# The shift-vector add of the first two layer norms issued on Pool instead of the Vector engine

## The chip, the cores and the metric

One Trainium2 chip, eight NeuronCores. Every core runs the same program on its own two sequences of the batch of sixteen; no data passes between cores. The metric is device time in microseconds (us) of the slowest core. PE is the matrix engine (PEld its weight loads), DVE the Vector engine, ACT the Scalar engine, Pool the GpSimd engine, SP the engine whose queue carries most DMAs.

## The reference

One layer of a streaming encoder, width 1024, sequences of 2048 tokens. Cut to what matters:

```python
def layer_norm(x, g, b):
    mu = mean(x, -1); var = mean((x - mu) ** 2, -1)
    return (x - mu) * rsqrt(var + EPS) * g + b          # b is the shift vector

h = x
mix = hybrid_mixer(h)          # in-projection, attention heads | SSD heads, then W_out
h = layer_norm(ALPHA * h + mix, ln1_g, ln1_b)
xa = memory_cross_attention(h, mem)                     # 4 heads over 256 memory tokens
h = layer_norm(ALPHA * h + xa, ln2_g, ln2_b)
ffn = hierarchical_moe(h)      # top-1 group, top-2 experts of it
h = layer_norm(ALPHA * h + ffn, ln3_g, ln3_b)
```

## The kernel before

Each core takes its two sequences one after the other through four stages: the in-projection with its convolutions (called P2 in the code's names), attention and SSD scan together (P3 to P5), the out-projection with the first normalisation (P6), and cross-attention with the second normalisation and the router (P7). The expert stage for both sequences together and the third normalisation follow. A sequence is 16 tiles of 128 tokens, and a tile of the residual is 128 partitions x 1024 float32 in `arenaH`; the gain vector `lng` and the shift vector `lnb` lie in SBUF, repeated on all partitions.

Every engine works through its own queue in the order in which the Python program emits instructions. That order is set by generators: a tile is a generator that emits a few instructions and yields, and a loop advances each living generator once per round. Waits are set by a small tracker (`Sched`): each tile of memory has a token that knows its last writer and its readers, and an instruction waits for the semaphore counts of those on other engines.

**P6.** A new tile (`p6_tile`, lines 1224 to 1240) starts every third round. Its steps, one a round: 16 matmuls of 128x512 into two PSUM banks (L1229), residual plus product (DVE, L1233), two statistics and their aggregate (DVE, L1195 to L1197), two tiny activations that make the reciprocal deviation (ACT, L388 and L389), a tiny negated mean (DVE, L1201), the normalisation itself (ACT, L1204), times `lng` (DVE, L1206), plus `lnb` (DVE, L1208), a cast to bf16 (ACT, L1238), eight transposes (PE, L1213), a copy into `actT` (ACT, L1216). So four tiles n-3 to n are in work at once. In three rounds the queues receive, in this order:

- DVE: multiply of tile n-2, add of n-2, negated mean of n-1, residual of n, statistics of n
- ACT: reciprocal deviation of n-1, copy of n-3, cast of n-2, normalisation of n-1
- PE: transposes of n-3, matmuls of n

**P7.** A cross-attention unit of one head and 512 tokens (`xa_unit`) starts every ninth round, 16 a sequence. Once the four units of a group of tokens are done, its four tiles go through `xa_tail`, one begun every ninth round: two halves of 8 matmuls each (L1334), residual (DVE, L1338), the same normalisation steps, cast (ACT, L1343), DMAs of the tile on SP's queue, transposes (PE, L1213), router logits (PE, L1350), some 25 small DVE instructions (L1353 to L1395) that choose experts and positions, and two indirect DMAs on Pool's queue (L123) that wait for the last of them (L1395). In PE's queue the transposes of a tile stand before the second half of the matmuls of the next tile. Small DVE instructions of the tile before stand between the residual of a tile and its multiply, and others (L1377 to L1395) behind its add. In the first sequence the last four tiles run beside the first part of the second sequence's in-projection.

Pool's queue holds no compute in these stages. In P6 of the first sequence `cast_step` puts one DRAM-to-DRAM weight DMA into it every sixth round, which waits for all matmuls emitted so far; in P7 it holds the two indirect DMAs of each tile.

Of the kernel before, what the change touches and what calls it, by code (L numbers as in the profile page):

```python
# [9 lines left out]
ALU = mybir.AluOpType  # L10
# [140 lines left out]
def build(n_seq=2, stop_after=None, dumps=()):  # L151
    nc = bass.Bass("TRN2", target_bir_lowering=False)
# [61 lines left out]
    with es:  # L214
        S = Sched(nc, es)

        def sb(name, shape, dt):
            return es.enter_context(nc.sbuf_tensor(name, list(shape), dt))
# [10 lines left out]
        lnb = sb("lnb", [128, D], F32)  # L229
# [29 lines left out]
        tLN = T()  # L259
# [127 lines left out]
        def rstd_from(dst, src, scale, reads, writes, eps=EPS):  # L387
            S.op("act", reads, writes, lambda: nc.scalar.activation(out=dst, in_=src, func=AF.Ln, scale=scale, bias=eps))  # L388
            S.op("act", [], writes, lambda: nc.scalar.activation(out=dst, in_=dst, func=AF.Exp, scale=-0.5))  # L389
# [284 lines left out]
        for s in range(n_seq):  # L674
# [513 lines left out]
            def norm_steps(hap, tHt):  # L1188
                j_ = lnstate["i"] % 8
                lnstate["i"] += 1  # L1190
                tS = tLNS[j_]
                base = j_ * 16
                st, mv = lnst[:, base:base + 12], lnst[:, base + 12:base + 14]
                rs, nm = lnst[:, base + 14:base + 15], lnst[:, base + 15:base + 16]
                S.op("dve", [tHt], [tS], lambda: nc.vector.bn_stats(out=st[:, 0:6], in_=hap[:, 0:512]))  # L1195
                S.op("dve", [tHt], [tS], lambda: nc.vector.bn_stats(out=st[:, 6:12], in_=hap[:, 512:1024]))
                S.op("dve", [], [tS], lambda: nc.vector.bn_aggr(out=mv, in_=st))  # L1197
                yield
                rstd_from(rs, mv[:, 1:2], 1.0, [tS], [tS])
                yield  # L1200
                S.op("dve", [tS], [tS], lambda: nc.vector.scalar_tensor_tensor(  # L1201
                    out=nm, in0=mv[:, 0:1], scalar=-1.0, in1=rs, op0=ALU.mult, op1=ALU.mult))
                yield
                S.op("act", [tS], [tHt], lambda: nc.scalar.activation(out=hap, in_=hap, func=AF.Identity, scale=rs, bias=nm))  # L1204
                yield
                S.op("dve", [tLN], [tHt], lambda: nc.vector.tensor_tensor(out=hap, in0=hap, in1=lng[:], op=ALU.mult))  # L1206
                yield
                S.op("dve", [tLN], [tHt], lambda: nc.vector.tensor_tensor(out=hap, in0=hap, in1=lnb[:], op=ALU.add))  # L1208
                yield

            def trans_steps(hb, tHB, tt):
# [13 lines left out]
            def p6_tile(tt):  # L1225
                tok = slice(tt * 128, (tt + 1) * 128)
                hap = hview[:, tt, :]
                bm = yield from bank2()
                S.op("pe", tCat + tWoL, bm.toks, lambda: [nc.tensor.matmul(  # L1229
                    bm.ap[:, hf * 512:(hf + 1) * 512], catT[:, c, tok], wout_k(c)[:, hf * 512:(hf + 1) * 512],  # L1230
                    start=(c == 0), stop=(c == 7)) for hf in range(2) for c in range(8)])
                yield
                S.op("dve", bm.toks, [tH[tt]], lambda: nc.vector.scalar_tensor_tensor(  # L1233
                    out=hap, in0=hap, scalar=ALPHA, in1=bm.ap, op0=ALU.mult, op1=ALU.add))
                psrel(bm)
                yield
                yield from norm_steps(hap, tH[tt])
                S.op("act", [tH[tt]], [tHbP[tt % 2]], lambda: nc.scalar.copy(out=hbP[tt % 2], in_=hap))  # L1238
                yield
                yield from trans_steps(hbP[tt % 2], tHbP[tt % 2], tt)  # L1240
# [72 lines left out]
            def xa_tail(tt):  # L1313
# [26 lines left out]
                psrel(bm)  # L1340
                yield
                yield from norm_steps(hap, tHt)
                S.op("act", [tHt], [tHB], lambda: nc.scalar.copy(out=hb, in_=hap))  # L1343
                S.dma("sp", out=XB[gt * 128:(gt + 1) * 128, :], in_=hb, reads=[tHB])
# [115 lines left out]
        if stop_after is None:  # L1460
            while webq:
# [20 lines left out]
                                        in1=thr[:].unsqueeze(1).to_broadcast([128, 32, 32]), op=ALU.is_gt))  # L1482
# [168 lines left out]
            for ti in range(NTI):  # L1651
# [15 lines left out]
                if ti == 4:  # L1667
                    pq(lambda: V_.tensor_tensor(out=tmpP, in0=RK[:].unsqueeze(2).to_broadcast([128, GT * 2, 32]),
                                                in1=ecap[:].unsqueeze(1).to_broadcast([128, GT * 2, 32]), op=ALU.is_ge))
# [143 lines left out]
```

How the kernel before makes its waits and increments, by code:

```python
    def _wait(self, eng, key, val):  # L75
        if self.seen.get((eng, key), 0) >= val:
            return
        self.eng[eng].wait_ge(self._semof(key), val)
        self.seen[(eng, key)] = val
# [14 lines left out]
    def op(self, eng, reads, writes, emit):  # L94
        need = self._need(eng, reads, writes)
        keys = list(need)
        attach = keys[-1] if keys else None
        for k in keys[:-1]:
            self._wait(eng, k, need[k])
        r = emit()
        first, last = (r[0], r[-1]) if isinstance(r, list) else (r, r)
        if attach is not None:
            first._wait_ge(self._semof(attach), need[attach])
            self.seen[(eng, attach)] = need[attach]
        self.cnt[eng] += 1
        last.then_inc(self.sem[eng], 1)
        self._commit((eng, self.cnt[eng]), reads, writes)
# [1 line left out]
    def dma(self, q, out, in_, reads=(), writes=(), out_off=None, in_off=None, bound=None, slots=None, cond=None):  # L109
# [12 lines left out]
            bound = self.bregs[bound]  # L122
            inst = self.nc.gpsimd.indirect_dma_start(
                out=out, out_offset=None if out_off is None else bass.IndirectOffsetOnAxis(ap=out_off, axis=0),
                in_=in_, in_offset=None if in_off is None else bass.IndirectOffsetOnAxis(ap=in_off, axis=0),
                bounds_check=bound, oob_is_err=False)
        inst.then_inc(self.dsem[slot], 16)
        self.dcnt[slot] += 16
        self._commit((slot, self.dcnt[slot]), reads, writes)
```

## Time and profile before

| | us |
|---|---|
| median of 3 runs | 2559.43 |
| the three runs | 2599.96, 2559.43, 2555.1 |
| the profiled execution's own time | 2549.81 |
| its span on the slowest core (core 5) | 2548.7 |
| spans of the eight cores | 2504.4 to 2548.7 |

A span runs from the first to the last instruction of a core. Rows of the trace are from core 5. A timeline row is: start, duration, engine, source line, operation, what it writes <- what it reads, shape, how many instructions are merged; in brackets how long the engine had been idle before and what released it. PE durations are modelled.

### The profile page before, as it was taken

How to read it: one execution, taken by the hardware profiler on the slowest of the kernel's cores; microseconds unless marked ns; L12 is line 12 of the kernel's file. 1: busy time of each engine (PE TensorE's matmuls, PEld its weight loads, DVE VectorE, ACT ScalarE, POOL GpSimd, SP SyncE). 2: the span in 40 equal slices, each digit the busy share in tenths (PEclk: the TensorE clock that was granted, in tenths of full speed). 3: DMA queues.
4: the chain of work that ended last, by engine and by line, in shares of the span. 5: the costliest groups of instructions: out<-in, count | busy, mean ns of one | idle time of the engine just before them, and what ended most of it. 6: DMA issues, size and time to landing. Idle time of an engine off the chain costs nothing.

```text
span 2548.7 us, 36342 instructions; the slowest of 8 cores (2504.4 to 2548.7 us)
## 1 busy us (share of the span) xinstructions
PE 1913.7 (75%) x10088; PEld 831.9 (33%) x10088; DVE 1607.1 (63%) x3781; ACT 1340.8 (53%) x2754; POOL 355.7 (14%) x411
## 2 busy tenths in 40 slices
PE   3886777878778865877778777788734899999674
PEld 1333223432333332433224332333312333333221
DVE  2567877874857866679768663948874322222199
ACT  1564677778555533665777775655521333333233
POOL 1021000001000110100000010001111222222361
PEclk9897788988999987987789888999966999999898
DMA  8399914537961142641546559110005768851584
GB/s 186 74 108 109 110 26 65 89 54 131 200 99 50 63 109 75 99 59 18 66 62 96 75 67 232 47 44 22 21 18 209 268 233 265 286 178 59 160 294 181
DMA packets 201709, 293.44 MB, mean 115 GB/s; under 512 B 55924, under 2 KB 136308, under 8 KB 196368
## 3 DMA queue, kind: packets, MB, share of 16 engines
q0 software_dynamic: 102944, 110.12, 29.9%
q1 hardware_dynamic: 83456, 155.87, 19.1%
q10 hardware_dynamic: 15120, 25.14, 2.6%
q8 instruction: 94, 1.54, 0.3%
q14 instruction: 95, 0.78, 0.1%
HBM read 421.38 MB, written 129.65 MB: 216 GB/s over the span
## 4 chain that ended last, share of the span: by engine, by line
DVE 38%; PE 35%; ACT 13%; issue 6%; DMA 5%; SPq 2%; another core or an unknown queue 0%; DVEq 0%; POOL 0%; ACTq 0%; POOLq 0%
PE ps L1615 8%; PE ps L484 5%; ACT arenaA L819 4%; DVE arenaKW L576 4%; PE ps L1631 4%; PE ps L1334 3%; DVE arenaH L1208 3%; DVE arenaH L1206 2%; PE ps L811 2%; PE ps L832 2%; PE ps L1609 2%; ACT arenaKW L916 2%; DVE hbs L576 2%; SPq L118 2%; PE ps L1278 2%
## 5 line engine op out<-in xcount | busy, mean ns | idle before, releaser
L819 ACT ACTIVATE arenaA<-ps 128x512 bf16<-128x512 f32 (+3 forms) x640 | 317.5, 535 | 35.3 <-PE ps L832 26.2
L811 PE MATMUL ps<-arenaA 96*128 96x512 bf16 (+3 forms) x640 | 252.2, 398 | 76.2 <-ACT arenaA L819 34.9
L484 PE MATMUL ps<-arenaA,arenaKW 128*128 128x512 bf16 (+1 forms) x1088 | 260.2, 401 | 42.5 <-DVE arenaA L496 20.8
L832 PE MATMUL ps<-arenaA 128*128 128x512 bf16 (+3 forms) x640 | 248.9, 393 | 40.9 <-DVE arenaA L822 21.0
L1615 PE MATMUL ps<-arenaKW 128*128 x760 | 247.8, 382 | 10.9 <-DMA arenaKW<-WEB 8.8
L1619 DVE TENSOR_TENSOR arenaKW<-arenaKW,ps 128x256 bf16<-128x256 f32 x95 | 40.0, 421 | 260.5 <-ACT arenaKW L1618 257.4
L484 PEld LDWEIGHTS ps<-arenaA,arenaKW 128*128 128x128 bf16 (+1 forms) x1088 | 113.5, 106 | 177.7 <-issue 36.2
L123 POOL DMA_INDIRECT IDX<-tokg,posX x64 | 63.2, 987 | 596.0 <-DVE posX L1395 547.0
L123 POOL DMA_INDIRECT arenaKW<-XB,xidx x95 | 95.5, 1006 | 342.3 <-PE ps L1609 314.3
L1618 ACT ACTIVATE arenaKW<-ps 128x256 f32<-128x256 f32 x95 | 36.4, 383 | 186.3 <-PE ps L1615 186.3
L1334 PE MATMUL ps<-arenaKW 128*128 128x512 bf16 x512 | 131.8, 404 | 1.0 <-issue 0.5
L811 PEld LDWEIGHTS ps<-arenaA 96*128 96x128 bf16 x640 | 68.7, 108 | 190.3 <-ACT arenaA L819 78.7
L1229 PE MATMUL ps<-arenaKW 128*128 128x512 bf16 x512 | 120.7, 392 | 6.1 <-DVE arenaKW L800 6.1
L1615 PEld LDWEIGHTS ps<-arenaKW 128*128 128x128 bf16 x760 | 72.9, 96 | 159.5 <-issue 147.6
L1635 ACT ACTIVATE arenaA<-ps,xgate 128x1024 bf16<-128x1024 f32 x63 | 70.2, 1114 | 97.0 <-PE ps L1631 92.0
L576 DVE SCALAR_TENSOR_TENSOR arenaKW<-arenaKW,convw_s 128x512 f32<-128x512 f32 x132 | 98.7, 750 | 34.6 <-ACT arenaKW L573 31.5
L1278 PE MATMUL ps<-arenaA,arenaKW 128*128 128x512 bf16 x512 | 117.3, 382 | 0.0
L1631 PE MATMUL ps<-arenaKW 128*128 x380 | 115.7, 379 | 2.0 <-DVE arenaKW L1626 0.8
L832 PEld LDWEIGHTS ps<-arenaA 128*128 128x128 bf16 x640 | 66.6, 104 | 131.6 <-DVE arenaA L822 46.0
L916 ACT ACTIVATE arenaKW<-arenaKW,small 128x128 f32<-128x128 f32 x256 | 102.1, 399 | 4.5
L822 DVE MEMSET arenaA<- 64x64 bf16 x256 | 28.3, 112 | 120.3 <-ACT arenaA L819 111.4
L388 ACT ACTIVATE lnst<-lnst 128x1 f32<-128x1 f32 x96 | 19.5, 203 | 151.8 <-DVE lnst L1197 75.0
(327 smaller groups left out, 4009.5 us busy)
## 6 DMA issues: line engine op xcount, KB each, us to landing
arenaKW<-WEB SPq DMA_DIRECT2D x99, 1536.0 KB
WEB<-wg POOLq DMA_DIRECT2D x32, 512.0 KB, 6.4
WEB<-wu POOLq DMA_DIRECT2D x32, 512.0 KB, 6.3
WEB<-wd POOLq DMA_DIRECT2D x32, 512.0 KB, 6.0
arenaH<-x SPq DMA_DIRECT2D x32, 512.0 KB
YS<-arenaA ACTq DMA_DIRECT2D x63, 256.0 KB
H2D<-arenaH SPq DMA_DIRECT2D x16, 512.0 KB
YS<-arenaKW ACTq DMA_DIRECT2D x32, 256.0 KB
```

The source lines that it names most:

```text
L123: inst = self.nc.gpsimd.indirect_dma_start(out=out, out_offset=None if out_off is None else bass.IndirectOffsetOnAxis(ap=out_off, axis=0), ...
L484: S.op("pe", list(tXT[tg * 4:tg * 4 + 4]) + [tWinL[wt]], bank_.toks, lambda: [nc.tensor.matmul(bank_.ap[0:M, :], lhs_fn(k), actT[:, k, tg ...
L576: S.op("dve", [tp, tC], [ta], lambda: nc.vector.scalar_tensor_tensor(out=a_, in0=p_[:, j:j + 512], scalar=convw[:, c * 4 + j:c * 4 + j + 1 ...
L811: S.op("pe", [tQ[hp], tK[hp]], b_.toks, lambda: nc.tensor.matmul(b_.ap[:, c0:512], kT[hp][0:96, kj * 128:(kj + 1) * 128], qT[hp][0:96, g * ...
L819: S.op("act", b_.toks, [tpt], lambda: nc.scalar.activation(out=pt[:, c0:512], in_=b_.ap[:, c0:512], func=AF.Exp, scale=SCALE))
L832: S.op("pe", [tpt, tV[hp]], bo.toks, lambda: nc.tensor.matmul(bo.ap[:, c0:512], Vaug[hp][:, kj, :], pt[:, c0:512], start=(kj == 0), stop=( ...
L916: S.op("act", [tE, tSm2], [tE], lambda: nc.scalar.activation(out=E[:, hh * 128:(hh + 1) * 128], in_=E[:, hh * 128:(hh + 1) * 128], func=AF ...
L1229: S.op("pe", tCat + tWoL, bm.toks, lambda: [nc.tensor.matmul(bm.ap[:, hf * 512:(hf + 1) * 512], catT[:, c, tok], wout_k(c)[:, hf * 512:(hf ...
L1278: S.op("pe", tHT[tg * 4:tg * 4 + 4] + tWq, bq_.toks, lambda: [nc.tensor.matmul(bq_.ap, wq[:, k, c * 128:(c + 1) * 128], actT[:, k, cols], ...
L1334: S.op("pe", [tXo[par]] + tWk, bm.toks, lambda: [nc.tensor.matmul(bm.ap[:, hf * 512:(hf + 1) * 512], xo_[:, c, j * 128:(j + 1) * 128], wou ...
L1615: S.op("pe", [tXst[ti % 3], tLd[95 + ti] if ti < 5 else tLd[ti - 4]], bg.toks, lambda: [nc.tensor.matmul(bg.ap, xst[ti % 3][:, k, :], KW[: ...
L1631: S.op("pe", [tHt_[i], tUse[ti]], bd2.toks, lambda: [nc.tensor.matmul(bd2.ap[:, hf * 512:(hf + 1) * 512], hdT[i][:, fc, :], KW[:, bass.ds( ...
```

## The change

The add of `lnb` in `norm_steps`, which P6 and P7 both use, is issued on Pool's queue and done by Pool. The multiply before it stays on DVE and the cast after it on ACT. Nothing else in the program text moves; the waits of what reads the tile are now for Pool's semaphore. The third normalisation has its own code and is untouched.

```diff
@@ norm_steps
                 S.op("dve", [tLN], [tHt], lambda: nc.vector.tensor_tensor(out=hap, in0=hap, in1=lng[:], op=ALU.mult))
                 yield
-                S.op("dve", [tLN], [tHt], lambda: nc.vector.tensor_tensor(out=hap, in0=hap, in1=lnb[:], op=ALU.add))
+                S.op("pool", [tLN], [tHt], lambda: nc.gpsimd.tensor_tensor(out=hap, in0=hap, in1=lnb[:], op=ALU.add))
                 yield
```

## Rows read from the trace of the kernel before

**Rows 1.** The page's busy times: engine, busy us (share), instructions.
```profile
PE 1913.7 (75%) x10088; PEld 831.9 (33%) x10088; DVE 1607.1 (63%) x3781; ACT 1340.8 (53%) x2754; POOL 355.7 (14%) x411
```

**Rows 2.** The page's chain that ended last, by line.
```profile
PE ps L1615 8%; PE ps L484 5%; ACT arenaA L819 4%; DVE arenaKW L576 4%; PE ps L1631 4%; PE ps L1334 3%; DVE arenaH L1208 3%; DVE arenaH L1206 2%; PE ps L811 2%; PE ps L832 2%; PE ps L1609 2%; ACT arenaKW L916 2%; DVE hbs L576 2%; SPq L118 2%; PE ps L1278 2%
```

**Rows 3.** The add by stretch: count, ns min/median/max, first and last start.
```profile
L1208 DVE TENSOR_TENSOR arenaH<-arenaH,lnb x16: 1224/1224/1226, 655.4 to 734.2; 128x1024 f32<-128x1024 f32 x16
...
L1208 DVE TENSOR_TENSOR arenaH<-arenaH,lnb x16: 1224/1225/1226, 1579.4 to 1661.2; 128x1024 f32<-128x1024 f32 x16
...
L1208 DVE TENSOR_TENSOR arenaH<-arenaH,lnb x12: 1224/1225/1226, 777.8 to 914.8; 128x1024 f32<-128x1024 f32 x12
...
L1208 DVE TENSOR_TENSOR arenaH<-arenaH,lnb x16: 1218/1224/1226, 777.8 to 1007.0; 128x1024 f32<-128x1024 f32 x16
...
L1208 DVE TENSOR_TENSOR arenaH<-arenaH,lnb x16: 1224/1225/1227, 1703.7 to 1890.2; 128x1024 f32<-128x1024 f32 x16
```

**Rows 4.** Windows, P6 then P7: length, busy PE PEld DVE ACT POOL, clock, DMA.
```profile
643.50:725.50 82.00, 64.25 (x361) 30.02 (x360) 75.11 (x104) 47.49 (x71) 5.75 (x7) 0.99 1.04 181
...
770.00:893.00 123.00, 102.32 (x592) 46.10 (x590) 103.18 (x320) 71.43 (x137) 15.80 (x16) 1.00 0.15 59
```

**Rows 5.** Timeline of P6, somewhat over one period of one tile.
```profile
680.70 1.17 DVE L1206 TENSOR_TENSOR arenaH<-arenaH,lng 128x1024 f32<-128x1024 f32 x1
...
681.90 1.22 DVE L1208 TENSOR_TENSOR arenaH<-arenaH,lnb 128x1024 f32<-128x1024 f32 x1
...
683.12 1.22 DVE L1233 SCALAR_TENSOR_TENSOR arenaH<-arenaH,ps 128x1024 f32<-128x1024 f32 x1
683.16 1.04 ACT L1238 CAST hbs<-arenaH 128x1024 bf16<-128x1024 f32 x1 [1.00 <-DVE arenaH L1208]
...
684.11 1.24 ACT L1204 ACTIVATE arenaH<-arenaH,lnst 128x1024 f32<-128x1024 f32 x1
...
684.26 0.62 PE L1213 MATMUL ps<-ident_bf,hbs 128*128 128x128 bf16 x8 [1.25 <-ACT hbs L1238]
...
684.72 3.62 PE L1229 MATMUL ps<-arenaKW 128*128 128x512 bf16 x16
...
685.96 1.17 DVE L1206 TENSOR_TENSOR arenaH<-arenaH,lng 128x1024 f32<-128x1024 f32 x1
...
688.31 0.15 DVE L1201 SCALAR_TENSOR_TENSOR lnst<-lnst 128x1 f32<-128x1 f32 x1
...
688.44 1.22 DVE L1233 SCALAR_TENSOR_TENSOR arenaH<-arenaH,ps 128x1024 f32<-128x1024 f32 x1
```

**Rows 6.** Timeline of P6's end: the last two multiplies.
```profile
728.30 1.17 DVE L1206 TENSOR_TENSOR arenaH<-arenaH,lng 128x1024 f32<-128x1024 f32 x1
...
732.98 1.23 DVE L1206 TENSOR_TENSOR arenaH<-arenaH,lng 128x1024 f32<-128x1024 f32 x1 [2.19 <-ACT arenaH L1204]
```

**Rows 7.** Timeline of P7, from one tile's multiply to the next tile's.
```profile
826.25 1.22 DVE L1206 TENSOR_TENSOR arenaH<-arenaH,lng 128x1024 f32<-128x1024 f32 x1
...
827.50 1.23 DVE L1208 TENSOR_TENSOR arenaH<-arenaH,lnb 128x1024 f32<-128x1024 f32 x1
...
828.81 1.05 ACT L1343 CAST arenaKW<-arenaH 128x1024 bf16<-128x1024 f32 x1 [2.04 <-DVE small L1377]
...
829.91 0.62 PE L1213 MATMUL ps<-ident_bf,arenaKW 128*128 128x128 bf16 x8 [0.42 <-ACT arenaKW L1343]
...
830.37 1.89 PE L1334 MATMUL ps<-arenaKW 128*128 128x512 bf16 x8
...
831.52 0.17 DVE L1395 CAST posX<-RK 128x2 int32<-128x2 f32 x1
...
832.29 1.22 DVE L1338 SCALAR_TENSOR_TENSOR arenaH<-arenaH,ps 128x1024 f32<-128x1024 f32 x1 [0.60 <-PE ps L1334]
...
832.68 0.98 POOL L123 DMA_INDIRECT IDX<-tokg,posX  x1 [10.30 <-DVE posX L1395]
...
838.71 1.22 DVE L1206 TENSOR_TENSOR arenaH<-arenaH,lng 128x1024 f32<-128x1024 f32 x1
```

## The prediction

> **What bounds the kernel now.** I read the page's busy times first: Pool is busy 14% of the span, DVE 63% [rows 1]. That says there is room on Pool and nothing of what the room is worth. The chain that ended last has the add itself on it: L1208 holds 3% of the span, the multiply before it 2% [rows 2]. I then looked for the adds line by line. There are 64 of 1.225 us: two lots of 16 in P6 and two of 16 in P7 [rows 3]. The windows give the shares there: in P6 DVE is busy 75.1 of 82 us and PE 64.3; in P7 PE 102.3 and DVE 103.2 of 123 [rows 4]. So DVE looks like P6's limit, and P7 has two engines at 84% with neither full. The timelines decide, because the add lies between two other engines: what comes after it (ACT's cast, PE's transposes) stands in queues ahead of the work on which the next tile depends.
>
> In P6 one period is 685.96 - 680.70 = 5.26 us, and 5.32 in turn: 10.58 for two. Three circuits run through it [rows 5].
> - DVE alone: multiply, add, negated mean, residual, statistics; nearly full, 5.3.
> - Circuit A: multiply 680.70, add, cast 683.16, normalisation 684.11 to 685.35 (ACT has the cast of the older tile ahead of it), next multiply. Where DVE isn't in its way at the end of P6, this circuit shows by itself: 728.30 to 732.98 is **4.68**, with DVE idle 2.19 us waiting for ACT [rows 6].
> - Circuit B, over two periods: cast 683.16, transposes 684.26, matmuls 684.72 to 688.34, residual 688.44 (5.28 us so far); residual to next multiply 685.96 - 683.12 = 2.84; multiply to cast 683.16 - 680.70 = 2.46. The sum is 10.58, or **5.29** a tile. The matmuls end at 688.34, between the starts of the negated mean (688.31) and of the residual (688.44): PE is exactly as late as DVE.
>
> In P7 the period is 838.71 - 826.25 = **12.46** us, and one circuit fills it [rows 7]: multiply 826.25, add 827.50, cast 828.81, transposes 829.91, second half of the next tile's matmuls 830.37 to 832.26, residual 832.29, then 6.42 us of DVE work to the next multiply. The small DVE instructions behind the add end at 831.69 (L1395), and DVE is idle 0.60 before the residual: it waits for PE.
>
> **The change, part by part.**
>
> *DVE's add goes.* It frees 1.225 us a tile, 64 times. In P6 the circuit of DVE alone falls to about 4.1, but B stays at 5.29 and A at 4.68 even if Pool were as quick. In P7 the add's place on DVE was followed by small instructions that wait anyway. So the relief alone is worth nothing; PE's lateness covers it.
>
> *Pool's add comes.* No row shows Pool computing on a tile. From below: DVE's add of the same shape, 1.225 us [rows 3]. From above: two passes over the tile, one for each operand, 2 x 1.225 = 2.45, and on top the slowest hand-over to Pool in these rows, 831.69 to 832.68 = 0.99 for an indirect DMA [rows 7], so 3.44. I take 2.45 with hand-overs of 0.05 on both sides, like the one from DVE's add to ACT's cast (683.12 to 683.16 [rows 5]). Nothing in the rows says that Pool matches DVE, so I go by the two passes and not by the lower end; the hand-over I take from compute engines, since the 0.99 belongs to a DMA with its set-up.
> The GPSIMD Engine Reference of the Trainium skill (section 3.1, Elementwise) has the two-input float32 add at 1.96 times DVE's time, since Pool's two operands share one read port; its own Pool figure is 4497 ns for 2048 columns. By that ratio the add would be an estimated 2.40 us and the sum below about 2 us smaller; no row here shows it.
>
> *What it does to the step from multiply to cast.* Now 2.46 in P6 and 2.56 in P7. After: 1.17 to 1.22 + 0.05 + 2.45 + 0.05 = 3.72 to 3.77. That is **1.25 us more** (1.26 and 1.21).
>
> *P6.* A becomes 4.68 + 1.25 = 5.93, B (10.58 + 1.25)/2 = 5.92. Both pass DVE. A gap grows by 0.64. A sequence has 15 gaps between its 16 multiplies; 14 grow by 0.64, the last one by 1.25 since it runs at 4.68 now, and the last tile's cast comes another 1.25 later: 9.0 + 1.25 + 1.25 = 11.5. Two sequences: **+23**. In the second sequence two early gaps wait for other things and may hide a little of it; I take 22.
>
> *P7.* All of the step is in the circuit, so each tile pays 1.25. First sequence: 12 adds from 777.8 to 914.8 in the regular rhythm; the other four, up to 1007.0, lie among the in-projection of the next sequence, where I count two of them. Second sequence: 16 [rows 3]. 30 x 1.25 = **+37.5**.
>
> *What is queued behind.* Pool's indirect DMAs of a tile (832.68, 0.98 each) are done long before the next tile's multiply ends (839.9), so the add does not wait for them; those issued after it have 4 us of room. P6's weight DMAs on Pool in the first sequence wait for matmuls that are older than the multiply in question; 7 of them take 5.75 us in 82 [rows 4] and fall between adds. I cost both at nothing; if that cover were gone, a DMA's 1 us would be added in every second tile of one P6, 8 us. SP's DMAs of the tile follow the cast or the add by its 1.25 and wait for nothing else. ACT has room: 47.5 of 82 us.
>
> *The clock.* It is 0.99 and 1.00 of the 2.4 GHz level in these windows, with PE 78% and 83% busy. PE's share falls to about 70% and 76%. If the granted clock went to 0.9, the matmuls and transposes in the circuits (4.1 us in P6, half of it per tile; 2.4 in P7) would give 0.2 x 30 + 0.27 x 30 = 14 us. I count none and keep it for the range.
>
> Sum: 22 + 37.5 = 59.5 on the profiled execution's 2549.8, thus 2609. The median of the runs is 9.6 above that execution, the fastest run 5.3, so I put a median of runs 5 above it: **2614 us**, which is 2.3% more than 2554.8, the execution of before with the same 5. The times of the rivals below are on the execution's own footing, without the 5.
>
> **The rivals.**
>
> *Not slower: Pool as quick as DVE (chance 0.07).* If an add on Pool takes 1.25 or less from hand-over to hand-over, the step from multiply to cast doesn't grow. P7 stays. P6 stays too if B binds; if PE could in truth start its matmuls earlier, P6 falls to A's 4.68, 0.61 x 30 = -18 us: 2532 to 2550. It decides at an add of 1.2 us. For it: Pool has nothing else to do. Against it: none; it is only unmeasured.
>
> *In between (0.13).* Pool takes 1.7 to 2.1 us with hand-overs. Each 0.1 us costs 0.05 x 30 in P6 until A takes over, 0.1 x 30 in P7 and some at the ends, 4.7 us in all. With hand-overs 1.7 to 2.1 us means a step longer by 0.4 to 0.8, 19 to 38 us: 2569 to 2588.
>
> *A much longer Pool step (0.10).* At the upper bound 3.44 the step grows by 2.2: P6 by 1.6 x 28 + 9 = 53, P7 by 66, together 2669. What speaks for it is that hand-overs to Pool are the slowest in these rows; against it, that all of them are DMAs.
>
> *DVE shut out while Pool works (0.10).* DVE's negated mean in P6 comes right behind the multiply. If it could not run beside Pool's add, DVE's circuit would be multiply 1.17, the add with its hand-over 2.5, negated mean 0.15, residual and statistics 2.84: 6.66 instead of 5.93, 0.73 x 30 = 22 more, 2631. Against it: it starts some 0.1 before the multiply's end now (688.31 [rows 5]), so it is in before Pool can start. In P7 the small instructions behind the add take 3.1 us and have 3.5 until the residual, so nothing comes of it there.
> This is the rule of SBUF — State Buffer in the Trainium skill (Who interferes with whom): a DVE instruction with two SBUF inputs and a Pool instruction that reads SBUF share one read port, and the later of the two waits for the whole of the other. No row here shows the two together.
>
> **How the numbers follow.** Forecast 0.60: a step longer by 1.0 to 1.6 us, which is 2597 to 2629 and 2602 to 2634 as medians. With the rivals: 0.07 not slower, 0.13 in between, 0.10 shut out, 0.10 longer. The range leaves out the not-slower case, the lower half of the middle one and the upper end of the longer one: **2582 to 2655**. 2% is what a measurement here can tell from no change, 51 us; the forecast crosses it at a step longer by 1.1 (4.7 for each 0.1). Of the forecast's 0.60 I put 0.42 above it, and all of the last two rivals: slower 0.62. Within 2%: 0.18 + 0.13 + 0.04 = 0.35. Faster by over 2% would need P6 and P7 both to shed the DVE time: 0.03.
>
> **What would show it.** In P6 the multiply would come every 5.9 us, DVE would be idle before it with ACT's normalisation as the releaser, and DVE's busy share would drop from 92% to about 70%. The cast would wait for Pool in every tile. In P7 the multiply would come every 13.7 us, PE idle before the transposes 1.2 us more, DVE idle before the residual about 1.8. A period of 5.3 and 12.5 with a Pool add of over 2 us would prove the circuits wrong; an add of 1.3 us only its price. A negated mean that starts when Pool's add ends would show the shut-out.

## The result, and the profile after

Medians of the runs that stand beside each other: 2633.18 us with the change (four runs, 2619.46 to 2653.89), 2561.11 us before (four runs, 2555.1 to 2599.96). The ratio is **1.029**, with a 95% interval of 1.025 to 1.033: slower by 72 us. One of the four runs with the change had one die at a lower clock; it is in the medians and not in the ratio. The forecast was 2614 us. The profiled execution took 2628.91 us, its longest span is 2627.8 us on core 4, and the rows below are from that core.

The busy times of the page after (the row that answers to [rows 1]):

```profile
PE 1947.4 (74%) x10088; PEld 838.5 (32%) x10088; DVE 1589.6 (60%) x3717; ACT 1339.4 (51%) x2754; POOL 507.1 (19%) x475
```

64 instructions have gone from DVE, which is busy only 17.5 us less, although 64 adds of 1.225 us (78 us) left it: something else on DVE has become longer by 60 us. Pool has 64 more instructions and 151.4 us more. PE does the same 10088 instructions and is busy 33.7 us longer. The groups of instructions name DVE's part (busy us, mean ns of one, idle time before it):

```profile
L1378 DVE TENSOR_TENSOR small<-small 128x1 f32<-128x1 f32 x32 | 62.0, 1936 | 1.1
```

Before, these 32 took 0.159 us each, 5 in all: 57 of the 60 us. Over the eight cores 213 of them ran while Pool's add did, and every one ended with it.

In the chain of waits by line Pool's L1208 holds 4%, where DVE's held 3% [rows 2]. The answer for line L1208, which stands against [rows 3]: duration as min/median/max in ns, and who waited for it (us, times).

```profile
L1208 POOL TENSOR_TENSOR arenaH<-arenaH,lnb x64: 2328/2342/2363, 668.1 to 1967.6; 128x1024 f32<-128x1024 f32 x64
...
  ACT hbs L1238: 79.3, 32
  ACT hbs L1343: 54.1, 15
  ACT arenaKW L1343: 47.8, 15
```

The add takes 2.34 us on Pool, 1.91 times DVE's 1.225. ACT waits for Pool before 62 of the 64 casts: the sum is hardly ever ready early.

The windows after (columns as in [rows 4]): P6, a short one inside it, and P7:

```profile
666.00:737.00 71.00, 47.84 (x240) 21.48 (x240) 42.65 (x63) 34.79 (x51) 29.78 (x16) 0.86 0.88 160
700.00:702.00 2.00, 2.00 (x7) 0.71 (x6) 1.29 (x2) 1.30 (x4) 0.56 (x1) 0.51 1.03 170
...
800.00:885.00 85.00, 66.03 (x379) 29.56 (x378) 66.50 (x181) 44.85 (x84) 24.06 (x16) 1.00 0.15 57
```

In P6 DVE falls from 92% to 60% and PE from 78% to 67%; the granted clock falls from 0.99 to 0.86, while P7 keeps 1.00. The short window shows 0.51 from 700 to 702 us; from 706 to 708 us the same view says 1.00.

The timeline of P6 over two periods, against [rows 5]:

```profile
694.28 1.17 DVE L1206 TENSOR_TENSOR arenaH<-arenaH,lng 128x1024 f32<-128x1024 f32 x1
695.37 0.15 DVE L1201 SCALAR_TENSOR_TENSOR lnst<-lnst 128x1 f32<-128x1 f32 x1
695.54 2.34 POOL L1208 TENSOR_TENSOR arenaH<-arenaH,lnb 128x1024 f32<-128x1024 f32 x1 [2.66 <-DVE lnst L1201]
695.66 1.22 DVE L1233 SCALAR_TENSOR_TENSOR arenaH<-arenaH,ps 128x1024 f32<-128x1024 f32 x1
697.91 1.04 ACT L1238 CAST hbs<-arenaH 128x1024 bf16<-128x1024 f32 x1 [2.18 <-POOL arenaH L1208]
...
699.02 0.62 PE L1213 MATMUL ps<-ident_bf,hbs 128*128 128x128 bf16 x8 [3.46 <-ACT hbs L1238]
...
699.47 5.30 PE L1229 MATMUL ps<-arenaKW 128*128 128x512 bf16 x16
700.14 1.23 DVE L1206 TENSOR_TENSOR arenaH<-arenaH,lng 128x1024 f32<-128x1024 f32 x1 [1.56 <-ACT arenaH L1204]
...
705.37 3.62 PE L1229 MATMUL ps<-arenaKW 128*128 128x512 bf16 x16
707.72 1.17 DVE L1206 TENSOR_TENSOR arenaH<-arenaH,lng 128x1024 f32<-128x1024 f32 x1
```

Multiply to cast is 697.91 - 694.28 = 3.63 us, 1.17 more than before. The two gaps between multiplies are 5.86 and **7.58** us, 13.44 for two where 10.58 + 1.17 = 11.75 would follow from the step alone. The other 1.69 us are in one row: after PE had waited 3.46 us for a cast, its 16 matmuls took 5.30 us, and the same 16 took 3.62 a period later. The clock in that stretch is the 0.51 of the window: PE at its lower level, 1.2 GHz. Ten such gaps in this core's P6 stages, at 1.68 us each, are half of PE's 33.7 us.

The same wait does not always end so. Two such pairs later, on this core:

```profile
725.89 0.62 PE L1213 MATMUL ps<-ident_bf,hbs 128*128 128x128 bf16 x8 [3.46 <-ACT hbs L1238]
726.35 3.62 PE L1229 MATMUL ps<-arenaKW 128*128 128x512 bf16 x16
```

From there on the stage keeps its full clock, PE waits 1.83 us before every tile's transposes, and the gaps are 5.91. Over the eight cores the first group behind the late start of a stage (PE idle 4.3 to 12.8 us) was slow in all 16 stages (4.9 to 6.1 us); after it, 41 of 56 waits of 3.4 to 3.8 us were followed by a slow group, and none of the 80 waits of 1.83. In the kernel before, 8 of the 16 stages had one or two such long gaps at their start (6.6 to 7.9 us), and then none.

The timeline of P7 from one multiply to the next, against [rows 7]:

```profile
834.46 1.22 DVE L1206 TENSOR_TENSOR arenaH<-arenaH,lng 128x1024 f32<-128x1024 f32 x1
...
835.76 2.34 POOL L1208 TENSOR_TENSOR arenaH<-arenaH,lnb 128x1024 f32<-128x1024 f32 x1 [5.37 <-DVE small L1377]
835.77 2.35 DVE L1378 TENSOR_TENSOR small<-small 128x1 f32<-128x1 f32 x1
838.14 1.04 ACT L1343 CAST hbs<-arenaH 128x1024 bf16<-128x1024 f32 x1 [3.15 <-POOL arenaH L1208]
...
841.69 1.22 DVE L1338 SCALAR_TENSOR_TENSOR arenaH<-arenaH,ps 128x1024 f32<-128x1024 f32 x1 [0.85 <-PE ps L1334]
...
848.11 1.22 DVE L1206 TENSOR_TENSOR arenaH<-arenaH,lng 128x1024 f32<-128x1024 f32 x1
```

The gap is 13.65 us against 12.46; most of this stage's are 13.70, against 12.47. Here is the longer L1378 too: one element per partition, it lasts 2.35 us and ends with Pool's add. DVE is still idle 0.85 us before the residual, so this stands beside the path.

**Where the 72 us are.** Read off the first and last multiply (L1206) of each stage on every core in the two profiled executions, medians of the eight cores, in us:

| stretch | before | after | difference | counted |
|---|---|---|---|---|
| span's start to the first multiply | 653.9 | 662.1 | +8 | 0 |
| P6, first sequence | 79.6 | 94.2 | +14.5 | +11 |
| P7, first sequence | 220.8 | 234.2 | +13.4 | +17.5 |
| last multiply to the second sequence's first | 566.8 | 568.5 | +2 | 0 |
| P6, second sequence | 79.9 | 96.7 | +17 | +11 |
| P7, second sequence | 186.6 | 205.1 | +18.5 | +20 |

Two switches from P6 to P7 add 2. The sum is 75, and 59.5 were counted.

### The profile page after: what moved, and what is told of

It is laid out like the page before. It is cut to its first block, busy times and chain, and to the rows that moved or that the text cites. A ratio compares the mean times of both kernels' runs of the same rounds, so it can differ in the third digit from the quotient of the medians.

```text
span 2627.8 us, 36387 instructions; the slowest of 8 cores (2577.8 to 2627.8 us)
## 1 busy us (share of the span) xinstructions
PE 1947.4 (74%) x10088; PEld 838.5 (32%) x10088; DVE 1589.6 (60%) x3717; ACT 1339.4 (51%) x2754; POOL 507.1 (19%) x475
## 4 chain that ended last, share of the span: by engine, by line
PE 37%; DVE 33%; ACT 13%; issue 5%; DMA 5%; POOL 4%; SPq 2%; another core or an unknown queue 1%; DVEq 0%; ACTq 0%; POOLq 0%
PE ps L1615 9%; PE ps L484 5%; POOL arenaH L1208 4%; PE ps L1631 4%; DVE arenaKW L576 3%; ACT arenaA L819 3%; PE ps L1334 3%; PE ps L1229 2%; SPq L118 2%; PE ps L1609 2%; DVE arenaH L1206 2%; PE ps L811 2%; ACT arenaKW L916 2%; PE ps L832 2%; DVE hbs L576 2%
## 5 line engine op out<-in xcount | busy, mean ns | idle before, releaser
L484 PE MATMUL ps<-arenaA,arenaKW 128*128 128x512 bf16 (+1 forms) x1088 | 278.4, 421 | 41.0 <-DVE arenaA L496 21.3
L1208 POOL TENSOR_TENSOR arenaH<-arenaH,lnb 128x1024 f32<-128x1024 f32 x64 | 149.9, 2343 | 410.8 <-DVE small L1377 156.6
L1229 PE MATMUL ps<-arenaKW 128*128 128x512 bf16 x512 | 134.9, 425 | 6.1 <-DVE arenaKW L800 6.1
L1334 PE MATMUL ps<-arenaKW 128*128 128x512 bf16 x512 | 134.3, 410 | 1.1 <-issue 0.7
L1618 ACT ACTIVATE arenaKW<-ps 128x256 f32<-128x256 f32 x95 | 36.4, 383 | 186.7 <-PE ps L1615 186.7
L811 PEld LDWEIGHTS ps<-arenaA 96*128 96x128 bf16 x640 | 68.7, 108 | 192.3 <-ACT arenaA L819 78.8
L1213 PE MATMUL ps<-ident_bf,hbs 128*128 128x128 bf16 x384 | 33.7, 238 | 99.3 <-ACT hbs L1238 64.4
```

The source lines that it names most:

```text
L484: S.op("pe", list(tXT[tg * 4:tg * 4 + 4]) + [tWinL[wt]], bank_.toks, lambda: [nc.tensor.matmul(bank_.ap[0:M, :], lhs_fn(k), actT[:, k, tg ...
L811: S.op("pe", [tQ[hp], tK[hp]], b_.toks, lambda: nc.tensor.matmul(b_.ap[:, c0:512], kT[hp][0:96, kj * 128:(kj + 1) * 128], qT[hp][0:96, g * ...
L1208: S.op("pool", [tLN], [tHt], lambda: nc.gpsimd.tensor_tensor(out=hap, in0=hap, in1=lnb[:], op=ALU.add))
L1229: S.op("pe", tCat + tWoL, bm.toks, lambda: [nc.tensor.matmul(bm.ap[:, hf * 512:(hf + 1) * 512], catT[:, c, tok], wout_k(c)[:, hf * 512:(hf ...
L1334: S.op("pe", [tXo[par]] + tWk, bm.toks, lambda: [nc.tensor.matmul(bm.ap[:, hf * 512:(hf + 1) * 512], xo_[:, c, j * 128:(j + 1) * 128], wou ...
```

## The experiments

**Each stage alone.** One kernel has Pool's add in P6 only, the other in P7 only:

```diff
-            def norm_steps(hap, tHt):
+            def norm_steps(hap, tHt, st_):
...
-                S.op("dve", [tLN], [tHt], lambda: nc.vector.tensor_tensor(out=hap, in0=hap, in1=lnb[:], op=ALU.add))
+                if st_ == 6:        # 7 in the second kernel
+                    S.op("pool", [tLN], [tHt], lambda: nc.gpsimd.tensor_tensor(out=hap, in0=hap, in1=lnb[:], op=ALU.add))
+                else:
+                    S.op("dve", [tLN], [tHt], lambda: nc.vector.tensor_tensor(out=hap, in0=hap, in1=lnb[:], op=ALU.add))
```

> The add of lnb is on Pool in the first normalisation (P6) only; P7's add stays on DVE. Circuit theory (what counts is the time from multiply to cast): the multiplies of P6 come every 5.9 us where PE's waits are even and 5.86 and 7.58 in turn where they are not, as in the changed kernel, P7 stays at 12.46; two P6 cost 12 to 20 us each, in all +25 to +40 us. Rival (DVE held up by the shared port wherever Pool works): in P6 no DVE instruction is stretched in the changed kernel, so under it P6 costs nothing and the whole loss stays with P7: 0 us here.

> The add is on Pool in the second normalisation (P7) only; P6 stays on DVE. Circuit theory: P7's multiplies come every 13.7 us instead of 12.46, P6 stays at 5.29; 11 gaps of 1.24 in the first sequence, 15 in the second and the last step, +32 to +36 us. Together with the P6-only kernel it should add up to the loss of both, 72 to 79 us. Rival (the two stages feed on each other, or the stages before P6 are slowed too): the two single kernels add up to clearly less than both.

P6 only: ratio 1.013 (1.003 to 1.023); P6 takes 91.4 to 99.6 us over the cores, P7 of the second sequence 186.7 to 189.9. P7 only: 1.013 (1.005 to 1.021); P6 78.8 to 82, the first eleven gaps of P7 149.9 us instead of 137.0, P7 of the second sequence 203.6 to 205.5. Each loss is in its own stage but for a little: with Pool in P6 only, P7's first eleven gaps take 138.1 to 141.5 us, since up to three of them are 13.6 or so (matmuls at the lower clock) and the others are 0.07 us longer. 1.3% + 1.3% make up the 2.9% within the intervals. The slow P6 gaps are there without any change in P7.

**A shorter Pool step.** Pool adds the first half of the columns; the other half of the shift is left out.

```diff
-                S.op("dve", [tLN], [tHt], lambda: nc.vector.tensor_tensor(out=hap, in0=hap, in1=lnb[:], op=ALU.add))
+                S.op("pool", [tLN], [tHt], lambda: nc.gpsimd.tensor_tensor(out=hap[:, 0:512], in0=hap[:, 0:512], in1=lnb[:, 0:512], op=ALU.add))
```

> Pool adds only columns 0 to 511 of the shift vector in both normalisations, and nothing adds the other half: half of the shift is left out. Pool's step should be about 1.2 us, as long as DVE's whole add, while DVE is relieved of all 1.225 us. Circuit theory: the time from multiply to cast is what it was, so P6 stays at 5.29 by circuit B and P7 at 12.46: no change within 5 us. Rival (DVE is the limit of P6, as its 92% say): P6 falls to circuit A's 4.68, 0.6 x 30 = 18 us faster. Second rival (Pool beside DVE costs by contention whatever the length of the step): slower by 10 us or more.

Timeline of this kernel in P6 (core 1):

```profile
696.25 1.17 DVE L1206 TENSOR_TENSOR arenaH<-arenaH,lng 128x1024 f32<-128x1024 f32 x1
697.51 1.26 POOL L1208 TENSOR_TENSOR arenaH<-arenaH,lnb 128x512 f32<-128x512 f32 x1 [2.67 <-DVE lnst L1201]
701.09 1.17 DVE L1206 TENSOR_TENSOR arenaH<-arenaH,lng 128x1024 f32<-128x1024 f32 x1
...
706.92 1.17 DVE L1206 TENSOR_TENSOR arenaH<-arenaH,lng 128x1024 f32<-128x1024 f32 x1
```

Pool takes 1.26 us here, what DVE's whole add took. Two gaps are 4.84 and 5.83, 10.67 together against 10.58 before, and the ratio is 1.005 (0.996 to 1.014). The step from multiply to cast is 0.09 us longer than before (2.55 and 2.46), and half of that is what the mean gap has grown by. DVE has lost its 64 adds and nothing is won: P6 shows the step "the relief alone is worth nothing" by itself, and the 18 us that the rival in the expectation asked for (0.993) lie outside the interval. P7 is no pure case of it: L1378 lasts 1.27 us beside the half add, the gaps are 12.62 instead of 12.47 with a few of 13.63, and the second sequence's P7 takes 188.6 to 191.2 us, before 186.1 to 186.9.

**The add left out** (no shift is added in P6 and P7):

> The add of the shift vector is left out of both normalisations altogether. Circuit theory: the step from multiply to cast is 1.25 us shorter, so P7 goes from 12.46 to 11.2 and P6 from 5.29 to (10.58 - 1.25)/2 = 4.67: 0.62 x 30 + 1.25 x 27 = 52 us faster. If only DVE's load counted, P6 would fall to 4.2 or to PE's own 4.2 and P7 by nothing, since DVE waits there: 33 us faster.

```diff
-                S.op("dve", [tLN], [tHt], lambda: nc.vector.tensor_tensor(out=hap, in0=hap, in1=lnb[:], op=ALU.add))
```

Ratio 0.991 (0.980 to 1.001), so a gain of the whole is not clear of the noise, and the 52 us expected are at the interval's very edge. P6 comes out as expected: 70.7 us where it is undisturbed, 4.71 a gap. P7 does not: its first eleven gaps take 131.2 us on six of the cores (135.5 on two), where 11.2 a gap had been expected, and the timeline of one gap (core 1) says why it isn't less:

```profile
802.86 0.20 PE L1373 MATMUL ps<-ONE,su_bf 128*128 128x64 bf16 x1 [1.45 <-DVE ONE L1367]
...
802.91 1.22 DVE L1206 TENSOR_TENSOR arenaH<-arenaH,lng 128x1024 f32<-128x1024 f32 x1
...
804.16 1.05 ACT L1342 CAST hbs<-arenaH 128x1024 bf16<-128x1024 f32 x1 [0.72 <-DVE arenaH L1206]
...
806.00 0.61 PE L1212 MATMUL ps<-ident_bf,hbs 128*128 128x128 bf16 x8
...
814.79 1.22 DVE L1206 TENSOR_TENSOR arenaH<-arenaH,lng 128x1024 f32<-128x1024 f32 x1
```

The gap is 11.88, not 12.46 - 1.25 = 11.2. The cast ends at 805.21 and the transposes start at 806.00 with PE never idle between: PE's own work (L1333 and L1285 of other tiles), which hangs on DVE's router result (L1367) and on its queue, is the next circuit, 0.6 us behind the first. So with all else as it is, no treatment of this add should win more than its absence does: 8 us in each P6 and 6 to 7 in each P7.

**PE's wait filled.** The changed kernel, with seven matmuls that compute nothing of use before each tile's transposes in P6:

```diff
-            def trans_steps(hb, tHB, tt):
+            def trans_steps(hb, tHB, tt, fill=0):
                 pb = yield from bank()
+                if fill:
+                    S.op("pe", [tC] + tWoL, pb.toks, lambda: [nc.tensor.matmul(
+                        pb.ap, ident_bf[:], wout_k(0)[:, 0:512], start=True, stop=True) for _ in range(fill)])
...
-                yield from trans_steps(hbP[tt % 2], tHbP[tt % 2], tt)
+                yield from trans_steps(hbP[tt % 2], tHbP[tt % 2], tt, 7)
```

> The changed kernel with seven extra 128x512 matmuls in P6 ahead of each tile's transposes, into the bank that the transposes then overwrite; they run while PE waits for the cast. Clock theory: the gaps of 7.58 us come from PE standing idle 3.46 us, after which its clock is at the lower level for most of a tile's 16 matmuls (5.30 us instead of 3.62). With the wait filled no group takes 5.3, all gaps are 5.9, and P6 takes 89 us a sequence from first to last multiply instead of 91 to 100; P7 stays at 13.7. Rival (the long gaps come from Pool's queue, where weight DMAs stand between the adds, or from DMA traffic): they stay.

Its timeline in P6 (core 0; L1216 are the transposes, L1232 the matmuls of the tile, L1214 the fillers):

```profile
700.57 1.22 DVE L1206 TENSOR_TENSOR arenaH<-arenaH,lng 128x1024 f32<-128x1024 f32 x1
...
703.36 1.67 PE L1214 MATMUL ps<-arenaKW,ident_bf 128*128 128x512 bf16 x7
...
705.36 0.62 PE L1216 MATMUL ps<-ident_bf,hbs 128*128 128x128 bf16 x8 [0.33 <-ACT hbs L1241]
...
705.81 3.62 PE L1232 MATMUL ps<-arenaKW 128*128 128x512 bf16 x16
706.48 1.23 DVE L1206 TENSOR_TENSOR arenaH<-arenaH,lng 128x1024 f32<-128x1024 f32 x1
```

The gap is 5.91 in every period from 671 us on until the last, and no group of 16 takes longer than 3.62. This is what was forecast for P6 (5.92), once the clock holds. So the alternation of 5.86 and 7.58 comes from the clock after PE's wait and not from a second circuit. The whole is no faster for it: 1.025 (1.017 to 1.032), P6 98.1 to 101 us and not the 89 expected, since the fillers stretch P6's end, where PE also has the first unit of P7: the last gap is 14.4 us on this core.

**Can Pool be used at all here?** ACT and PE need only the bf16 sum; the float32 sum is read much later. In four kernels DVE writes the bf16 sum directly (which leaves out ACT's cast), and Pool makes the float32 sum beside the path, at different places in P7:

```diff
+                    S.op("dve", [tLN, tHt], [tHB_], lambda: nc.vector.tensor_tensor(out=hb_, in0=hap, in1=lnb[:], op=ALU.add))
...
+            def pool_sum(hap, tHt):
+                S._wait("pool", "dve", S.cnt["dve"])
+                S.op("pool", [tLN], [tHt], lambda: nc.gpsimd.tensor_tensor(out=hap, in0=hap, in1=lnb[:], op=ALU.add))
...
-                yield from norm_steps(hap, tHt)
-                S.op("act", [tHt], [tHB], lambda: nc.scalar.copy(out=hb, in_=hap))
+                yield from norm_steps(hap, tHt, hb, tHB)
```

The call of `pool_sum` stands, in the first, a step behind the DMA of the bf16 tile, meant for the time of the next residual:

> P6 as before the change. In P7 DVE's sum is written as bf16 straight into the buffer that the transposes read, so ACT's cast leaves the path; the float32 sum that the residual needs is done by Pool off the path, issued so that it starts behind the next tile's residual on DVE, in a stretch of 4 us in which DVE has no instruction with two SBUF inputs. Circuit theory: the step from multiply to transposes is 1.05 us shorter, until the next circuit (PE's own, 11.93 us in the kernel without the adds) binds: P7 at 11.93 instead of 12.46, -13 us. Rival (Pool beside DVE costs whatever it does): P7 slower than 12.46.

in the second right behind the bf16 sum:

> The same as the kernel with the bf16 sum, but Pool's float32 sum is issued at once, right behind DVE's sum. Nobody on the path waits for it. Port theory: it starts beside DVE's small instructions, the first of these with two SBUF inputs (L1378 in the old numbering) lasts until Pool is done, 2.35 us, and pushes the rest of them and the next residual back: multiply to residual 7.9 us instead of 6.04, gaps in P7 of about 14.3 us, 2.4 more than with the late issue; +50 us against before. Rival (only waits for Pool's result cost time): the same time as with the late issue.

in the third as in the first, and P6 treated alike:

> The bf16 sum on DVE and the late float32 sum on Pool in both normalisations. P7 as with P7 alone, 11.93. In P6 circuits A and B lose the cast's 1.05 us (A 3.6, B 4.77), but DVE's own circuit stays at 5.29, since it has the same instructions: gaps of 5.29 and no gain there, except that a late start of P6 is made up sooner. -13 to -17 us in all. If Pool's add collides with DVE's multiply in P6 (2.34 us in a free stretch of 2.84), P6 gaps are up to 0.5 longer.

The ratios are 1.021 (1.016 to 1.027), 1.012 (1.006 to 1.018) and 1.025 (1.020 to 1.030). All three expectations failed, the first and the third by their sign, the second in its order: the sum issued at once costs less than the late one (30 us, and not 50). A sum that nobody waits for costs about as much as the change did in P7 (1.013), or more. Timeline and window of the first (core 7):

```profile
823.26 2.37 POOL L1216 TENSOR_TENSOR arenaH<-arenaH,lnb 128x1024 f32<-128x1024 f32 x1
825.03 0.64 DVE L1363 TENSOR_SCALAR small<-small 128x4 f32<-128x4 f32 x1
...
828.60 0.20 PE L1381 MATMUL ps<-ONE,su_bf 128*128 128x64 bf16 x1 [1.86 <-DVE ONE L1375]
```

```profile
829.80:831.80 2.00, 2.00 (x6) 0.74 (x5) 1.68 (x5) 0.58 (x1) 0.00 (x0) 0.50 0.00 0
```

DVE's L1363 takes 0.64 us instead of 0.23, up to the end of Pool's sum (825.63). With that the router's result comes later, PE waits 1.86 us for it instead of 1.45, and then works at a clock of 0.50: its eight matmuls take 3.39 us instead of 1.89. P7's gap is 14.0. (Of the waits of 1.76 to 1.90 us at this place, on all cores, 72 of 88 were followed by slow matmuls; of the 160 waits of 1.45 in the kernel before, none.) The second kernel (core 4) and the third (core 2) show the plainer forms:

```profile
834.33 2.35 POOL L1216 TENSOR_TENSOR arenaH<-arenaH,lnb 128x1024 f32<-128x1024 f32 x1 [6.96 <-DVE tokg L1389]
834.43 2.29 DVE L1393 TENSOR_TENSOR small<-small,ONE 128x32 f32<-128x32 f32 x1
```

```profile
703.93 2.35 POOL L1216 TENSOR_TENSOR arenaH<-arenaH,lnb 128x1024 f32<-128x1024 f32 x1 [3.69 <-DVE arenaH L1240]
705.40 1.96 DVE L1206 TENSOR_TENSOR arenaH<-arenaH,lng 128x1024 f32<-128x1024 f32 x1
```

An instruction of 0.19 us lasts 2.29, and P6's multiply 1.96 instead of 1.22; the last is on P6's path, whose gap is 6.04. In both kernels Pool's sum started a round later than I had meant: the semaphore it waits for counts DVE's whole queue up to the call.

In the fourth the sums are kept in a list and issued at the end of the next tail, where DVE does its residual (which reads PSUM) and its statistics:

> P6 as before. In P7 DVE's sum goes as bf16 straight into the buffer of the transposes, ACT's cast is gone, and Pool's float32 sum is issued ahead of the previous tile's indirect DMAs, so that it starts when that tile's last small DVE instruction is done and runs beside the residual and the statistics, none of which was stretched by Pool in any run so far; it should be over 0.3 us before the TENSOR_SCALAR that the late issue stretched from 0.23 to 0.64 us. Circuit theory: PE's wait before L1374 stays at 1.5 us, so its clock stays at the higher level, and P7's gap is 11.93 us against 12.46 before and 14.0 with the late issue: 131 us from the first to the twelfth multiply and 179 in the second sequence, -13 us in all, -0.5%. Rival (losing the cast upsets PE's order by itself): 13.5 to 14 again.

```diff
+                for ha_, th_, gt_ in pend:
+                    pool_sum(ha_, th_)
...
+                pend.clear()
```

Timeline (core 0):

```profile
815.97 1.22 DVE L1206 TENSOR_TENSOR arenaH<-arenaH,lng 128x1024 f32<-128x1024 f32 x1
...
821.69 2.36 POOL L1216 TENSOR_TENSOR arenaH<-arenaH,lnb 128x1024 f32<-128x1024 f32 x1 [8.89 <-DVE posX L1402]
...
827.86 1.22 DVE L1206 TENSOR_TENSOR arenaH<-arenaH,lng 128x1024 f32<-128x1024 f32 x1
```

Here nothing is held up (the residual, which starts at 821.45, takes 1.21 us) and the gap is 11.89, what leaving the add out gave. But the second and third gaps of a sequence are 13.16 and 13.56, there are more of 13.5 on most cores, and instead of the 13 us to be won the ratio is 1.003 (1.000 to 1.007).

**One sum for each tail**, so that no two are issued back to back:

```diff
-                for ha_, th_, gt_ in pend:
-                    pool_sum(ha_, th_)
...
+                pool_sum(hap, tHt)
```

> As e9, but each tile's tail issues its own float32 sum on Pool, one per tail, at its last step, ahead of its two indirect DMAs; there is no list from which two sums can come at once. If the two long gaps of e9 (13.15 and 13.57) came from two sums issued back to back at the end of the first tail, all P7 gaps are 11.9 us: 131 us for the first eleven gaps of the first sequence, 179 to 180 for the second sequence's P7, which is 6 + 7 = 13 us less than before, 0.5%, ratio 0.993 to 0.997. Rival: the long gaps have another cause (the start of P7 itself, which before doesn't show). Then they stay, P7 is 135 to 140 and 184 to 186 as in e9, and the ratio is 1.00. P6 is as before in both, 78.8 to 82.

This expectation failed: 1.006 (1.002 to 1.009). Gaps of 13.5 us still come, one to three a sequence; the third gap is one of them in 13 of 16 sequences, the others come at changing places. P7 of the second sequence is 182 to 185 us, before 186 to 187, and not 179 to 180. One such gap (core 4):

```profile
804.31 1.08 POOL L123 DMA_INDIRECT IDX<-tokg,posX  x1 [0.18 <-issue]
804.97 0.42 DVE L1360 TENSOR_SCALAR small<-small 128x4 f32<-128x4 f32 x1
...
808.32 0.20 PE L1378 MATMUL ps<-ONE,su_bf 128*128 128x64 bf16 x1 [1.65 <-DVE ONE L1372]
...
809.68 3.19 PE L1341 MATMUL ps<-arenaKW 128*128 128x512 bf16 x8
```

The same DVE instruction as in the first kernel is held, this time until Pool's indirect DMA ends (805.39). This DMA stood behind the sum in Pool's queue: the sum ends at 804.13, the DMA starts 0.18 us later. PE waits 1.65 us instead of 1.45 and its eight matmuls take 3.19 us. And there is a second loss: the time from the first sequence's last multiply to the second sequence's P6 is 575 to 591 us, before 562 to 576. SP's queue on core 0:

```profile
1038.88 0.32 SPq L118 DMA_DIRECT2D H2D<-arenaH  x1
1039.35 4.70 SPq L118 DMA_DIRECT2D arenaKW<-WINB  x3
```

The weight load of the second in-projection stands behind the transfer of the last residual tile, which waits for Pool's sum. It is issued 18.9 us after the last multiply (1020.46); before, 6.4. The answer for the in-projection's line, who ended the idle time there (us, times), of this kernel; it adds up the matmuls' and the weight loads' idle time, two records of the one wait, so PE stood still for about half of it, 22.6 us:

```profile
  DMA arenaKW<-WINB: 45.4, 2
```

**The last four tiles of the first sequence as before**, all else as in the kernel above:

```diff
+                old_ = s < n_seq - 1 and tt // 4 == gorder[-1]
+                if old_:
+                    yield from norm_steps(hap, tHt)
+                    S.op("act", [tHt], [tHB], lambda: nc.scalar.copy(out=hb, in_=hap))
+                else:
+                    yield from norm_steps(hap, tHt, hb, tHB)
```

> e10 gained 4.5 us in the second sequence's P7 and lost more between the last multiply of the first sequence's P7 and the second sequence's P6: 575 to 591 us in place of 562 to 576. Reading: the transfer of the last residual tile to DRAM waits for Pool's sum at the end of its tail and stands in SP's queue right ahead of the weight load of the second in-projection, which so is issued 18.9 us after the last multiply instead of 6.4 (core 0), and PE idles 35 to 45 us for it instead of 4 to 13. Here the last four tiles of the first sequence keep the two steps of before (sum on DVE in place, cast on ACT, transfer right behind it); the other 28 tiles are as in e10. If the reading is right, the weight load is issued about 6.4 us after the last multiply again, PE idles 4 to 13 us for it, the middle is 562 to 576 us, P7 of the second sequence stays 182 to 185, and the total is 4 to 6 us below before: ratio 0.997 to 1.000. Rival: the middle is longer since the first sequence's P7 ends at another point against the in-projection or because of the clock there. Then the middle stays at 575 to 590 and the ratio at 1.005.

The same answer of this kernel, same core:

```profile
  DMA arenaKW<-WINB: 4.3, 2
```

The load is issued 6.4 us after the last multiply, PE's own wait for it is 2.1 us, the stretch takes 558 to 577 us, P7 of the second sequence 181 to 184. The queue was the cause. (The 35 to 45 and 4 to 13 us of idle PE in the expectation are such double sums as well: PE's own waits were 16.6 to 22.6 us in the kernel above, and 1.9 to 6.7 before.) On three other cores PE still waits 8.4 to 9.5 us for the load, which I leave open. The ratio is 0.999 (0.997 to 1.002): the 4 to 6 us that I expected are within the interval and not shown. The stages say where they may have gone: the second sequence's P7 is 4 us shorter than before (medians 182.4 and 186.6), the first sequence's 6 us longer (226.9 and 220.8), most of it in the twelfth gap. Why that gap is longer is open. None of the kernels tried beats the one before.

## Why the prediction was right, and where it wasn't

**The direction and the mechanism held.** The add was on circuits that run through ACT and PE, so the relief of DVE paid nothing (the half add: 1.005, from 0.996 to 1.014) and the longer step was paid in full. Each stage's loss is in that stage but for a few us, by the two kernels that change one alone.

**The price of the Pool step.** Two passes, 2.45 us, against 2.34 measured; hand-overs of 0.05 against 0.09 (the multiply ends at 695.45, Pool starts at 695.54) and 0.03. The step from multiply to cast grew by 1.17 in P6, not 1.25, and by 1.12 in the rows of P7, not 1.21. The hand-over of 0.99 that made the upper bound belongs to the indirect DMA alone. The estimate of 2.40 us by the GPSIMD Engine Reference of the Trainium skill (section 3.1, Elementwise) is closer; the ratio to DVE is 1.91 here, 1.96 there for twice the columns.

**P7** was forecast at 13.71 us a gap and is 13.65 to 13.71. The sum came to 31.9 us instead of 37.5: the first sequence grew by 13.4 where 14 tiles had been counted (its first eleven gaps alone 13.6), so its last four tiles, two of which I had counted, cost nothing.

**P6 is the term that was mis-sized, by its clock.** Forecast 22 us, 2.5 of which fall behind the last multiplies, that is, into the switches; measured 31.4, and 2 in the switches. The gap by the circuits was right: 5.91, shown by the kernel with PE's wait filled. What failed is "I count none" for the clock. I had reasoned from PE's share of busy time and a clock of 0.9 spread evenly. The rows show something else: a full clock in most periods, and about half of it in matmuls that follow a PE wait of 3.46 us, in 41 of 56 cases. After a slow group PE waits 0.14 us for the next tile and 3.46 us again for the one after, so the alternation feeds itself until one such wait passes without a drop; how many periods that takes differs from stage to stage, and nothing here forecasts it. Each slow gap costs 7.58 - 5.91 = 1.67 us, and there are 3 to 10 of them in the 30 gaps of a core. For the core of the rows, 10 x 1.67 = 17 us, which with 2 x 10.2 from the step (the 11.5 without the last cast, which lies behind the last multiply) makes 37; its two P6 took 95.6 + 98.3, 36 more than the undisturbed 78.8 twice. The 14 us that I kept for the range were of the right size for the wrong reason: luck.

**What I hadn't in the sum at all** is 8 us before the first multiply, where the program is the same. Kernels with that same code have their first multiply at 651 to 671 us, so I take this as not the change's, without having shown it. The 2 us at the switches are of the size of the step (1.2 each). The 2 us in the middle I can't place: the last tile's transfer and the weight load behind it in SP's queue are 4.2 us later there (10.2 and 10.7 us after the multiply instead of 6.0 and 6.4), but PE waits no longer for that load than before (1.1 to 4.8 us against 1.9 to 6.7), and the eight cores of one kernel differ by more. So the total came out nearer than its terms: P6 was 9 to 11 us more than forecast and P7 6 less, which cancel in part by luck, and 8 of the 72 us are not shown to be the change's.

**The rivals.** *Not slower*, *in between* and *much longer* fell with the one row of 2.34 us. *DVE shut out* is half true. A DVE instruction that reads two operands from SBUF does wait for the end of Pool's add: L1378, 2.35 us for one element. That is nearly all of DVE's 60 us. But in the change it isn't on the path, as I had argued for both stages: in P6 the negated mean is in before Pool starts (695.37 and 695.54; the 688.31 that I had named for it lies before the end of the add, whose row isn't shown, and not of the multiply), in P7 the small instructions had room. How little room I hadn't seen: I expected 1.8 us of idle DVE before the residual, and 0.85 are left. The rule of SBUF — State Buffer in the Trainium skill (Who interferes with whom) is borne out, also in what it exempts: the residual, which has one input in PSUM, takes 1.22 us beside Pool's add (695.66), as it did without. Its form in the prediction, two SBUF inputs, doesn't cover the TENSOR_SCALAR with one that the experiments found held.

**A bound that was off.** At a step longer by 1.6 us circuit A (6.28) and not B binds P6, which makes P6 33 us and P7 48: 2631 where the prediction has 2629.

## What to carry to other kernels

An idle engine is a gain only for work that no other engine waits for, and here hardly even for that: write down the circuit on which the operation lies, put the new duration into it, and see what remains when the operation's time is nothing. Then ask how much longer the matrix engine will stand still in one piece after the change, and not what its mean share is: here the matmuls behind the longer waits often ran at half the clock, those behind the shorter ones at the same place never or seldom. Work taken off the path still holds ports and places in queues; look at what DVE does in that very time, and at what stands behind a transfer that now comes later.

## What the runs showed of the hardware

- A two-input DVE instruction of one element per partition lasted 2.35 us beside a Pool add, and ended with it; one of 32 elements 2.29. A DVE TENSOR_SCALAR of 4 elements with one float32 input was held too: 0.64 us instead of 0.23 beside Pool's add, 0.42 beside an indirect DMA (88 of the 211 that overlapped one there were longer, and each of these ended with it). The residual, with one input in PSUM, took 1.22 us with and without Pool.
- In P6 a PE wait of 3.46 us was followed by a granted clock of 0.51 and 16 matmuls of 5.30 us; waits of 3.4 to 3.8 us did so in 41 of 56 cases, waits of 1.83 us in none of 80. In P7 waits of 1.65 and 1.86 us were followed by a granted clock of 0.50 and by eight matmuls of 3.19 and 3.39 us instead of 1.89; waits of 1.76 to 1.90 us did so in 72 of 88 cases, those of 1.63 to 1.74 in the kernel with one sum for each tail in 29 of 57, those of 1.45 in none of 160 before the change and of 1.46 in 20 of 152 after it. So a longer wait made the lower clock likelier at the same place, and its length alone doesn't say what comes.
- The hand-over from DVE to a Pool compute instruction took 0.09 us, and from Pool to ACT 0.03, in P7 0.03 or 0.09.
